# Four stages of a two-layer trunk step reordered: the opening norm, attention scores, the odd layer's gates, and a modulation row in the mLSTM recurrence

## What is computed

```python
def sublayer(x, shift, scale, gate, g_pre, g_post, fn):
    h = rmsnorm(x, g_pre) * (1 + scale[:, None]) + shift[:, None]
    out, aux = fn(h)
    return x + gate[:, None] * rmsnorm(out, g_post), aux

# layer 0: projections, differential attention (4 heads) and
#          neighbourhood / dense attention (8 heads), out projection, dense SwiGLU (2816)
s = jnp.einsum('bqhmd,bkhmd->bhmqk', qb, k).astype(F32) * (A_HD ** -0.5)
p = jax.nn.softmax(s, axis=-1)
p = p[:, :, 0] - lam * p[:, :, 1]

# layer 1: odd_mixer, then a mixture of 8 experts, top 2
qk, v, o, gates, xd, gd = split(h @ w_in)
q, k = split(silu(conv_centred(qk, conv_c)))
hf, hb = mlstm_chunked(forward), mlstm_chunked(backward)      # 4 heads each
hc = rmsnorm(hf + flip(hb), norm_g) * sigmoid(o)
xc = conv_centred(xd, conv_d) + conv_d_b
hd = (rglru(xc, forward) + flip(rglru(flip(xc), backward))) * gelu(gd)
out = concatenate([hc, hd]) @ w_out
```

## Time and profile before

| | us |
|---|---|
| median of 3 runs (lowest to highest) | 1643.23 (1639.96 to 1644.5) |
| the profiled execution's own time | 1644.0 |
| its span in the trace | 1642.4 |
| PE busy | 1482.5 (90%) |
| DVE busy | 1061.1 (65%) |
| ACT busy | 890.9 (54%) |
| POOL busy | 98.2 (6%) |

### The profile page before, as it was taken

How to read it: one execution, slowest core, us unless ns; L and a number is a source line. 1 busy time by engine, 2 the same in 40 slices (tenths; PEclk the granted TensorE clock), 3 DMA queues, 4 the chain that set the end, 5 groups by cost and what they waited for, 6 DMA issues and landing times.

```text
span 1642.4 us, 19109 instructions
## 1 busy us (share of the span) xinstructions
PE 1482.5 (90%) x7385; PEld 1226.8 (75%) x7385; DVE 1061.1 (65%) x1289; ACT 890.9 (54%) x1040; POOL 98.2 (6%) x164
## 2 busy tenths in 40 slices
PE   4989798899999997995878799999999999999991
PEld 1987346799998877884456688888888888888881
DVE  1533545542324446587664698798987979879894
ACT  2422345543223344743245587687876867768773
POOL 0312400000000002010000200000000000000001
PEclk8999898999999998997989899999999999999996
DMA  9693981134342224222734699999999999999993
GB/s 361 183 406 111 326 304 55 57 99 153 103 151 106 103 78 167 103 66 101 247 125 173 265 351 392 358 406 369 396 389 373 403 376 385 393 363 404 379 384 131
DMA packets 146622, 414.52 MB, mean 252 GB/s; under 512 B 6925, under 2 KB 30889, under 8 KB 146409
## 3 DMA queue, kind: packets, MB, share of 16 engines
q1 hardware_dynamic: 134192, 375.93, 61.7%
q0 software_dynamic: 9600, 34.07, 5.7%
q10 hardware_dynamic: 2744, 3.36, 0.6%
HBM read 391.29 MB, written 22.95 MB: 252 GB/s over the span
## 4 chain that ended last, share of the span: by engine, by line
PE 79%; DVE 9%; ACT 5%; DMA 4%; issue 2%; POOL 1%; POOLq 0%; ACTq 0%; SPq 0%; DVEq 0%
PE bank L1788 38%; PE bank L1550 11%; PE bank L1561 6%; PE bank L1353 5%; PE bank L1402 4%; PE bank L1296 3%; PE bank L1350 3%; PE bank L1488 2%; DMA ring<-in_w_in_even_dram 1%; PE bank L1518 1%; PE bank L1756 1%; DMA ring<-in_mod_w_dram 1%; DVE arena L2151 1%; PE bank L1505 1%; PE bank L1320 1%
## 5 line engine op out<-in xcount | busy, mean ns | idle before, releaser
L1788 PE MATMUL bank<-arena_parts 128*128 128x512 f32 x1520 | 400.0, 391 | 0.9 <-DVE arena_parts L2420 0.9
L1788 PEld LDWEIGHTS bank<-arena_parts 128*128 128x128 f32 x1520 | 283.8, 188 | 62.2 <-issue 2.4
L2413 DVE TENSOR_TENSOR ring_parts<-ring,arena_parts 128x2048 fp32r<-128x2048 f32 x124 | 278.5, 2285 | 71.5 <-ACT arena_parts L1198 71.5
L1198 ACT ACTIVATE arena_parts<-ring 128x2048 fp32r<-128x2048 f32 x124 | 234.5, 1920 | 32.7 <-DMA ring<-in_moe_w_dram 31.4
L1788 PE MATMUL bank<-ring_parts,arena_parts 128*128 128x512 f32 x720 | 223.0, 391 | 0.0
L1788 PEld LDWEIGHTS bank<-ring_parts,arena_parts 128*128 128x128 f32 x720 | 135.7, 189 | 28.6
L1550 PE MATMUL bank<-ht_parts,arena_parts 128*128 128x384 f32 x352 | 118.3, 336 | 0.9 <-DVE xn_parts L1888 0.8
L1550 PE MATMUL bank<-ht_parts,ring_parts 128*128 128x384 f32 x352 | 117.7, 334 | 0.0
L1550 PE MATMUL bank<-xn_parts,arena_parts 128*128 128x384 f32 x352 | 117.7, 334 | 0.0
L1788 PE MATMUL bank<-xn_parts,arena_parts 128*128 128x512 f32 x320 | 93.8, 395 | 6.6 <-DVE ring_parts L2413 6.6
L1788 PE MATMUL bank<-ht_parts,arena_parts 128*128 128x512 f32 x320 | 94.1, 395 | 0.0
(11 more groups left out here) (423 smaller groups left out, 2697.1 us busy)
## 6 DMA issues: line engine op xcount, KB each, us to landing
ring<-in_moe_w_dram SPq DMA_DIRECT2D x184, 1024.0 KB, 7.0
arena<-in_moe_w_dram SPq DMA_DIRECT2D x60, 1024.0 KB, 6.9
ring<-in_mod_w_dram SPq DMA_DIRECT2D x24, 2048.0 KB, 8.8
ring<-in_ff_w_dram SPq DMA_DIRECT2D x23, 1024.0 KB, 7.8
ring<-in_w_in_even_dram SPq DMA_DIRECT2D x6, 2048.0 KB, 13.3
ring<-in_w_in_odd_dram SPq DMA_DIRECT2D x6, 2048.0 KB, 8.0
ring<-in_ff_w_dram SPq DMA_DIRECT2D x5, 2048.0 KB, 7.8
routed<-arena POOLq DMA_DIRECT2D x1, 7168.0 KB, 28.9
```

The costliest lines, as they stand in the source:

```text
L1198: act.activation(whi_moe[n_ % E_WHI], e_half(j, h), ACT.Copy).then_inc(whi_ready, 1)
L1788: ins = pe.matmul(bank[base + b][:, :], lhs[:, c_, :], rhs[:, k, 512 * b:512 * b + 512], start=(first and h == 0 and k == 0 and n_ == 0), ...
L2413: dve.tensor_tensor(e_half(j, h, low=True), e_half(j, h), whi_moe[(2 * j + h) % E_WHI], ALU.subtract).then_inc(wlo_ready, 1)
```

## The change

Six edits. Line numbers of the kernel after are higher than before's; the pairs are named where they matter.

1. Opening: ACT squares x and takes the root ahead of `keep_mod(1)`; DVE norms the rows ahead of `add_mod(0)` and `add_mod(1)`; PE issues `mod_mm(3)` ahead of all `turn_in`, and `mod_turn(3)` ahead of the last two.
2. Attention: `scores(i + 1)` in iteration i, with `scores(0)` ahead of the loop.
3. Gate weights: DVE's four copies into `wgp` move from behind the odd norm's halves into the FFN's down loop; ACT's `wgh` copy into `norm_in(1)`; the subtract that makes `wgl` moves from POOL to DVE.
4. Gates: their 48 matmuls come right behind the xd panel instead of behind k. DVE's log-sigmoid and scans are spread among low quarters over the gd and q panels. The row buffers move to other places in memory, which takes away a memset on POOL and makes DVE wait for the stores of the rows' last values before the first convolution of q. All copies of xd, q and k, and the first taps of the convolutions of xd and k, go to ACT. The `rg_mm` are cut in groups of four items and put inside and behind the panels.
5. o panel: PE turns k and issues `mlstm_logs(0)` ahead of its last quarter. ACT's sigmoids of o move behind unit 0's copies in the recurrence, and PE's `mod_mm(16)` waits for them. A subtract (`htl`) moves into DVE's unit 1.
6. Recurrence: ACT's `keep_mod(15+u)` stands behind `mlstm_exp(u+1)`.

```diff
@@ opening, ACT
             keep_mod(0)
-            keep_mod(1)
             for t in range(NT):
                 act.wait_ge(x_in, 32)
                 ins = act.activation(xn[:, t, :], x[:, t, :], ACT.Square, accum_out=ss[:, 0, t:t + 1])
             then(ins)
             act.activation(sd[:, 0, :], ss[:, 0, 0:3], ACT.Sqrt, scale=1.0 / D, bias=epsc[:, :]).then_inc(roots_ready, 1)
+            keep_mod(1)
             keep_mod(2)
             keep_mod(3)
@@ opening, DVE
-            add_mod(0)
-            add_mod(1)
             dve.wait_ge(roots_ready, 1)
             then(dve.reciprocal(rs[:, 0, :], sd[:, 0, :]))
             for t in range(NT):
                 normed_row(0, t)
+            add_mod(0)
+            add_mod(1)
@@ opening, PE
-            for k in range(4):
+            mod_mm(3)
+            for k in range(2):
                 turn_in(0, k)
-            mod_mm(3)
             mod_turn(3)
+            for k in range(2, 4):
+                turn_in(0, k)
@@ attention, PE
+            scores(0)
             for i in range(NU + 2):
+                if i + 1 < NU:
+                    scores(i + 1)
@@ odd projections, PE
             project(1, 0, "xd")
-            project(1, 1, "gd")
...
-            rg_mm(0)
-            project(1, 2, "q")
-            rg_mm(1)
-            project(1, 3, "k")
             pe.wait_ge(wgl_ready, 1)
...
+            project(1, 1, "gd", (nothing, nothing, lambda: rg_mm(0, 0)))
+            rg_mm(0, 4)
+            project(1, 2, "q")
+            rg_mm(1, 0)
...
+            project(1, 3, "k", (lambda: rg_mm(1, 4),))
+            project(1, 4, "v")
...
+            project(1, 5, "o", (nothing, nothing, first_logs))
+            pe.wait_ge(sw_ready, 1)
+            mlstm_logs(1)
+            mlstm_products(0)
+            for t in range(NT):
+                wait_kept(pe, index[("o", t)])
+            mod_mm(16)
@@ odd projections, DVE: the wait for the stores
+            low_quarters(13, 15)
+            dve.wait_ge(stored, 16 * 6)
+            conv_qk(0)
@@ recurrence, ACT
                 if u + 1 < 8:
                     mlstm_exp(u + 1)
+                if u:
+                    keep_mod(15 + u)
                 act.wait_ge(mm_done, u + 1)
...
-                keep_mod(16 + u)
                 act.wait_ge(cout_kept, u + 1)
                 act.dma_start(O[6][0, 0, d, h], cout[:, q, 0:P]).then_inc(c_stored[q], 16)
+                if u == 0:
+                    items_of("o", 0, 3)
+                    act.wait_ge(rg_free, 1)
+                    act.activation(hth[:, 4:8, :], gd[:, :, :], ACT.Copy).then_inc(ot_act, 1)
+            keep_mod(23)
```

More of the change, by code:

```diff
@@ L850, in norm_in @@
                         high_quarter(o, k // 2)
+                    if k == 3 and o == 1:
+                        act.wait_ge(wgp_ready, 4)
+                        act.activation(wgh, wgp[:, :, :, :], ACT.Copy).then_inc(wgh_ready, 1)
             def root_of_product(s, t):
@@ L1056, in _ @@
             norm_in(1)
-            act.wait_ge(wgp_ready, 4)
-            act.activation(wgh, wgp[:, :, :, :], ACT.Copy).then_inc(wgh_ready, 1)
             def odd_item(i):
@@ L1104, in rg_chain, with silu_of @@
                    .then_inc(rg_root, 1)
+            def silu_of(m):
+                act.wait_ge(conv_ready, m + 1)
+                act.activation(qkc[:, m, 1:1 + NPAD], qkc[:, m, 1:1 + NPAD], ACT.Silu).then_inc(qk_ready, 1)
             act.wait_ge(zeroed, 7)
-            def odd_panel(what, n0, n1):
-                for n_ in range(n0, n1):
-                    high_quarter(1, n_)
-                for i in range(len(even_items), len(items)):
-                    if items[i][0] == what:
-                        odd_item(i)
@@ new lines, in _ @@
+            items_of("xd", 0, 4)
+            high_quarters(6, 8)
+            act.wait_ge(soft_abs, 2)
+            act.activation(t2, rows[:, 1, :], ACT.Exp, scale=-1.0).then_inc(soft_exp, 1)
+            high_quarter(1, 8)
+            act.wait_ge(rates_ready, 2)
+            items_of("rg0", 0, 4)
+            high_quarter(1, 9)
+            items_of("rg0", 4, 8)
+            high_quarter(1, 10)
+            rg_gates(0)
+            high_quarter(1, 11)
+            items_of("gd", 0, 4)
+            high_quarter(1, 12)
@@ new lines, in _ @@
+            rg_decay(0)
+            items_of("q", 0, 4)
+            gate_exps()
+            high_quarters(13, 15)
+            items_of("rg1", 0, 4)
+            high_quarter(1, 15)
+            items_of("rg1", 4, 8)
+            rg_gates(1)
+            high_quarters(16, 18)
+            rg_decay(1)
+            items_of("k", 0, 4)
+            high_quarter(1, 18)
+            for m in range(4):
+                silu_of(m)
+            high_quarters(19, 21)
+            silu_of(4)
+            high_quarter(1, 21)
@@ L2247, in scan, with conv_x, conv_qk, low_quarters @@
                 then(ins)
+            ig, ff, t3, lf = (rows[:, k, :] for k in range(4))
+            def conv_x(m):
+                wait_kept(dve, index[("xd", m)])
+                conv(xc[:, m, :], xdin[:, m, :], col["conv_d"] + m, 4, True).then_inc(xc_ready, 1)
+            def conv_qk(m):
+                wait_kept(dve, index[("q" if m < 4 else "k", m % 4)])
+                conv(qkc[:, m, :], qkin[:, m, :], col["conv_c"] + m, 8, m >= 4).then_inc(conv_ready, 1)
+            def low_quarters(n0, n1):
+                for n_ in range(n0, n1):
+                    low_quarter(n_, 1)
@@ new lines, in _ @@
+            conv_x(0)
+            low_quarter(6, 1)
+            conv_x(1)
+            dve.wait_ge(gates_done, 1)
+            then(dve.tensor_scalar(ig, bank[4][0:36, 0:T], gbias[:, 0:1], None, ALU.add))
+            then(dve.tensor_scalar(t3, bank[5][0:36, 0:T], gbias[:, 1:2], None, ALU.add))
+            dve.scalar_tensor_tensor(out=ff, in0=t3, scalar=-1.0, in1=t3, op0=ALU.mult, op1=ALU.max)\
+               .then_inc(soft_abs, 1)
+            conv_x(2)
+            low_quarter(7, 1)
+            conv_x(3)
```

408 lines of the change are left out of this document (209 added, 199 removed).

## The result

The kernel after takes 1631.52 us (median of 5 runs, 1630.46 to 1633.1), against 1643.23 before: the ratio is 0.9928, with a 95% interval of 0.9908 to 0.9948. Its profiled execution spans 1630.6 us. The forecast was 1632. A "modulation matmul" is one `mod_mm`, a "turning" the transposes behind it; the recurrence's seven units are counted from its first modulation matmul to its eighth.

The account below looks back on a forecast made before the run. PE was taken as the bound, busy 90% of the span, so only its waits and lower clock could change. 1642.4 - 3.5 - 3.5 - 24.6 + 10.2 + 9.6 = 1630.6, plus 1.6 outside: 1632 us, range 1612 to 1650.

Parts of the forecast that it names:

- Recurrence: mLSTM recurrence, seven units: the copy behind the next exp lengthens each unit's chain, loss 10.2 us, plus 9.6 us of lower clock.
- The sign that I named: Recurrence, profile after: modulation matmuls at 1.92 us with waits of 2.5 ahead of them would take away 9.6 us.
- Odd projections: Odd layer's projections up to the recurrence's first modulation matmul: less waiting and lower-clock time on PE, gain 24.6 us (20 to 29).
- The sign "near 762": End of the odd projections, profile after: the recurrence's first modulation matmul would start near 762 us, against 786.25 before.
- Attention: Attention: scores issued one unit earlier start DVE's chain earlier and remove waits for exp, gain 3.5 us (0 to 8).
- so the lower clock behind them stays too: Attention: waits like the 2.25 us one stay for the greater part, and with them PE's lower clock.
- Opening: Opening: squares ahead of the second modulation row's copy bring the first projection to 38 to 39.2, gain 3.5 us (1.5 to 5).
- A plain shift of them: All later stages: they come out of a chain through PE, so an earlier stage's gain moves them by the same amount.
- No price in the recurrence: Rival, recurrence: the copy's new place is hidden, both loss terms of 20 us go, total 1612 us; chance 0.17.
- The gain lost on DVE: Rival, odd projections: the interleaved DVE queue makes low quarters late in turn, the last by 15 us, total 1647; chance 0.13.
- The clock staying down: Rival, recurrence: clock stays at the 1.2 GHz level through seven units of 12.4 or 15 us, total 1657; chance 0.10.
- Table loads: Skill page's rule: three loads on PE's path would each cost 1.4 us more, making the sum 4 us worse.

## Why the prediction was right, point by point

The time (1632 forecast, 1631.5 measured), the direction and the two large terms held. Below the sum not all did, and the half microsecond is luck.

- **Recurrence, -19.8 forecast, -19.5 measured.** The chain of matmul, logs, exp, copy, turning, products was right: with the clock held up the units take 7.6 to 8.0 and 8.6 us, forecast 8.1 and 8.75. I split the loss in 10.2 of chain and 9.6 of clock; by the traces it is 9.2 more idle and 10.3 more busy time. The runs correct the cause, though: the copy's place is 13.5 us of it in this kernel, and 6.0 come from the first two units, where the sigmoids and the subtract were moved. I had given these about 1 (9.15 for the first unit, measured 13.1). The other six, forecast at 46.65 and 9.6 for the clock, took 52.05. So the term hit because two errors of 4 us cancel. Of the 10.3 us more of busy time 4.0 are in the first unit and 6.3 in the six that I had given 9.6. The sign that I named failed too: I said that modulation matmuls at 1.92 would take away the clock's price, and most took 1.92 to 2.18, yet the price is there, in the products and turnings around them.
- **Odd projections, 24.6 forecast, 22.7 measured.** PE's work at the full clock plus 8 us of waits was the right way to sum: the waits are 4.5 (0.89, 1.04, 0.55, 1.98) and 4.34, forecast 4 and 4. The reason given for the first 4 was wrong: that DVE has 38.6 us idle. Its idle time lies where its inputs are missing. The doubled logarithm cost 7 us of the stage after and 9.9 before. That the change gained because the gate block no longer stands last fits the traces, but no run shows it by itself, and leaving the logarithm out of the kernel before gave only 5. The sign "near 762" for the recurrence's first modulation matmul left out the 7 us of the stages ahead; with them it is 754.6, and 754.98 was measured.
- **Attention, 3.5 forecast, 6.0 in the first pair of traces, 7.5 in the mean of fourteen profiles.** The step that failed is "so the lower clock behind them stays too". The waits did stay, 12.3 of 12.9, but the clock behind them went from 0.84 to 0.90, for a reason that stays open. The term came out near the upper end of its bounds.
- **Opening, 3.5 forecast, 3.9 in the pair of traces, 1.9 in the mean at the first projection, and 0 to 2.5 in the total.** The working followed the rows to within 0.7 us (root forecast at 22.7, it ran from 22.46 to 22.76; first projection 38 to 39.2, measured 38.8). What failed is the size: I had taken the term from one execution, with its first projection at 42.67, where seven profiles of the old opening spread over 3 us with a mean of 41.4. "A plain shift of them" holds on average: 1.9 us at the first projection and 2.3 at the start of attention. In the pair of traces half of it was gone there.
- These misses cancel. In the pair of traces the start of attention is 1.6 less ahead than forecast, and the projections gave 1.9 less. Against that attention gave 2.5 more, and the FFN, the recurrence and the rest 1.1 more. The sum was nearer than its parts.
- **The rivals.** No price in the recurrence: shown false, since the copy's new place alone costs 20 us in the kernel before and 13 to 15 in the kernel after. The gain lost on DVE: its mechanism (no slack in the queue) is real, its price wasn't. The clock staying down: it was 0.64 in the first unit and 0.82 over all, 0.83 to 0.96 in the others, never at the lower level throughout.
- **Table loads.** The Trainium skill's page "ScalarE: Activation LUTs", section "What ACT_TABLE_LOAD costs", would have added a drain of 1.38 us to each of three loads, 4 in all, an estimate. In the rows of the kernel with the sigmoids first the load follows the exp at once (745.17, 745.19) and the next activation starts 0.02 us behind it; nothing was added. The sum without it was the nearer one.

Two moves are a loss: the sixth edit, and in the fifth the place of the sigmoids. The kernel with the sixth edit undone and the sigmoids ahead of unit 1's exp takes 1610.4 us, 21 less than the kernel after (23 by the ratios) and 35 less than before. What is left there is the moved subtract (a wait of 2.84), which I didn't try apart.

## What to carry to other kernels

Follow a moved instruction to whoever waits for it through its new neighbour: a copy of 0.6 us put behind an exp cost 13 to 20 us, because the exp waits for an engine that waits for the copy's reader. Price a wait on the matrix engine twice, for its length and for the clock of the work behind it; filling 2.3 us of each wait with useless matmuls won 7.8 us of 65. And idle time of an engine is no slack by itself: double a suspected block and see. And take a term of 3 us from several executions or not at all.

## What was not expected of the hardware

The same work at the same place ran at either of the clock's two levels in different executions: the third modulation matmul of the opening took 1.92 or 3.64 us, and the last stretch of attention, in the old order, had a granted clock of 0.97 or 0.73. The spread went with the order of the work: with scores one unit ahead, eight profiles of attention lay within 0.9 us, without, six lay within 8.3. In the recurrence, units of 6 to 7.4 us with idles of 1.17 us had a clock of 1.00 but for the first, and the five behind the first with idles of 2.4 to 3.0, 8 to 10 us long, had 0.83 to 0.96.
